# Two-layer float32 block pair on one core: heads in pairs with row-tiled scores, spatial gating's last products moved into the heads' first steps

## The reference

```python
# first kind, l = 0, 1: beside a differential attention, eight heads of 64 over 1024 tokens, two key/value heads
q = apply_rope(rms_norm(bq)); k = apply_rope(rms_norm(bk))
ob = gqa_attention(q, k, bv)              # softmax(q k^T / 8) v, no mask, four query heads on one key head
yb = ob * silu(bg)

# second kind, l = 0, 1
y_a = silu(z_a) * (u * (einsum('gts,bcsgd->bctgd', tril(w_s), layer_norm(v)) + b_s))   # spatial gating
score = sum_h w_idx * relu(q_idx k_idx^T / 8)       # which keys a query may see
idx = top_k(score, 256)                             # ties go to the lower index
y_b = silu(z_b) * sparse_attention                  # eight heads of 64, one key/value head, the chosen keys only
```

## Time and profile before

| | us |
|---|---|
| median of the runs | 3182.53 (3180.21 to 3183.30, 3 runs) |
| profiled execution | 3185.18 |
| its span (first to last instruction) | 3183.4 |
| PE busy in the span | 2747.1 (86%) |
| DVE busy | 2070.8 (65%) |
| ACT busy | 1594.8 (50%) |
| POOL busy | 1154.7 (36%) |
| mean granted TensorE clock | 0.933 of full |
| unmasked heads, layers 0 and 1 | 569.1 to 785.9, 1431.8 to 1646.0 |
| end of the search and gating, layers 0 and 1 | 2152 to 2199, 2866 to 2912.5 |
| masked heads, layers 0 and 1 | 2199.0 to 2355.6, 2912.8 to 3070.5 |

### The profile page before, as it was taken

One profiled execution on the slowest core, in us unless ns is written; L12 is line 12 of the kernel. 1 busy time (PEld: TensorE's weight loads), 2 busy tenths in 40 slices (PEclk: granted clock), 3 DMA queues, 4 the chain that ended last, 5 costly groups with the idle time before them and its releaser, 6 DMA issues. The chain is left out here.

```text
span 3183.4 us, 40934 instructions
## 1 busy us (share of the span) xinstructions
PE 2747.1 (86%) x13680; PEld 2191.3 (69%) x13680; DVE 2070.8 (65%) x4254; ACT 1594.8 (50%) x3093; POOL 1154.7 (36%) x981
## 2 busy tenths in 40 slices
PE   6999798898979997889989797996889697996887
PEld 5877566677868775657777575775767575775766
DVE  4372387688434624858874348898867358898756
ACT  3221376688422114757873216674864316674861
POOL 0100277455001003864540001985631001985631
PEclk9999899899989997999999898998999899998989
DMA  4343110100324321001023100110022100110022
GB/s 123 118 137 103 73 39 7 40 1 28 119 72 144 123 70 54 24 5 39 1 72 108 53 20 24 47 44 24 1 110 76 63 24 17 47 44 24 1 87 80
DMA packets 90751, 181.92 MB, mean 57 GB/s; under 512 B 12552, under 2 KB 27912, under 8 KB 90504
## 3 DMA queue, kind: packets, MB, share of 16 engines
q1 hardware_dynamic: 74124, 150.69, 14.7%
q10 hardware_dynamic: 16416, 28.61, 3.0%
HBM read 149.87 MB, written 33.33 MB: 58 GB/s over the span
## 5 line engine op out<-in xcount | busy, mean ns | idle before, releaser
L681 PE MATMUL ps<-w_hi,hh 128*128 128x512 f32 (+1 forms) x640 | 243.1, 380 | 22.2 <-DVE w_lo L566 10.1
L1263 POOL TENSOR_SCALAR a_prob<-a_prob,a_ratio 128x1024 f32<-128x1024 f32 x64 | 72.1, 1126 | 505.5 <-DVE a_ratio L1222 505.5
L681 PE MATMUL ps<-w_lo,hh 128*128 128x512 f32 (+1 forms) x640 | 241.0, 377 | 0.0
L1685 PE MATMUL ps<-o_w_hi,hh 128*128 128x512 f32 x512 | 211.7, 414 | 32.2 <-DVE o_w_lo L1609 32.2
L681 PE MATMUL ps<-w_hi,hl 128*128 128x512 f32 (+1 forms) x640 | 239.3, 374 | 0.0
L2151 DVE TENSOR_SCALAR_CACHE_REDUCE select_rows<-masks,select_cuts 128x1024 bf16<-128x1024 int16 (+7 forms) x264 | 229.7, 873 | 0.2
L1685 PE MATMUL ps<-o_w_lo,hh 128*128 128x512 f32 x512 | 207.5, 405 | 0.0
L1685 PE MATMUL ps<-o_w_hi,hl 128*128 128x512 f32 x512 | 207.1, 405 | 0.0
L960 POOL TENSOR_SCALAR b_prob<-b_prob,b_recip 128x1024 f32<-128x1024 f32 x128 | 144.2, 1127 | 172.5 <-DVE b_recip L925 169.9
L1665 POOL TENSOR_TENSOR o_rstd<-o_rstd,nhalf 128x1 f32<-128x1 f32 x56 | 46.6, 833 | 423.8 <-DVE o_rstd L1546 245.3
L1211 DVE CUSTOM_DVE_ANT_0 a_prob<-ps,a_bias 128x1024 f32<-128x1024 f32 x128 | 151.6, 1222 | 57.9 <-PE ps L1348 57.9
(11 more groups left out here) (354 smaller groups left out, 8350.3 us busy)
## 6 DMA issues: line engine op xcount, KB each, us to landing
w_early<-in_w_in SPq DMA_DIRECT2D x108, 256.0 KB, 2.8
ada_w<-in_w_ada ACTq DMA_DIRECT2D x96, 256.0 KB, 2.7
w_raw<-in_w_in SPq DMA_DIRECT2D x84, 256.0 KB, 2.8
...
```

What stands on the lines that cost most here:

```text
L681: mm = nc.tensor.matmul(o, lhs, rhs, start=(k == 0 and i == 0), stop=(k == K - 1 and i == 2))
L1685: mm = nc.tensor.matmul(o, lhs, rhs, start=(k == 0 and i == 0), stop=(k == K - 1 and i == 2))
```

## The change

`heads_phase` now takes two heads at a time. The blocks of the two heads alternate: block g is query tile g%16//2 of head g%2 of its pair.

- Queries are turned as they lie (a tile of 128 columns holds both heads), keys are staged twice side by side by ACT; ACT writes the high half of the turned tile and DVE the low half, for both sides. So there are four query stacks instead of eight, and the staging of queries by ACT and DVE is gone.
- Scores of a pair of blocks: three products (high-high, high-low, low-high) for each head and bank with 64 rows each, heads in alternation: twelve instead of eight with 128 rows. Head 0 goes to banks 0 and 1, head 1 to banks 2 and 3. They are issued in odd steps for the next two blocks and wait until both blocks before are shifted.
- In the unmasked form too, DVE now writes the negated scores to SBUF (with a zero added in place of a mask), and ACT's exponential reads them there.
- `plan`: turned tiles start at step 4n+8 and stand only in even steps, all tiles of two steps together (four in a step, or two). With three banks the fourth turn of a step waits for the low half of the first. The ring holds 16 rows. A group is closed at step 4n+13 (4n+10 before), the loop ends at NB+14 (NB+11).

In `select_project_phase` the tie order is 3, 2, 7, 4, 6, 5, and the wait for the gates stands before the third; DVE multiplies chunk U from PSUM into the gates after the third (eight of 128x512), PE's spatial products follow, and ACT copies them into `v`. Bias and last product are given to `heads_phase` as `gating`: POOL does two products of 128x512 ahead of the scaling in each of its steps 1 to 8. `v` itself is lent as four rows of the ring, and DVE waits at block 12 until all eight gatings are done.

```diff
-    QB, RING, SLOTS, NS = 4, 10, 4, 4
+    QB, RING, SLOTS, NS = 4, 16, 4, 4
+    TURN, READ = 8, 13
...
         for j in range(tiles(n)):
-            plan[QB * n + 5 + j // per].append(("attn", n, j))
+            plan[QB * n + TURN + j // per // 2 * 2].append(("attn", n, j))
...
                 def shift(g):
-                    dve.wait_ge(scored, g + 1)
+                    dve.wait_ge(scored, g // 2 + 1)
...
+                    if g >= RING:
+                        dve.wait_ge(turned, last_tile[group_with(g - RING)])
+                    elif g == RING - len(lent):
+                        dve.wait_ge(mixed, len(gating))
+                    added = (row_view(bias(query_tile(g)), g) if causal
+                             else zero[:, 0:1].unsqueeze(2).broadcast_to([P, 2, BANK]))
+                    nc.vector.tensor_tensor_reduce(out=row_view(prob(g), g), in0=score_view(g), in1=added,
+                                                   scale=-1.0, scalar=3.0e38, op0=ALU.add, op1=ALU.min,
+                                                   accum_out=nm[:, g % NS:g % NS + 1]).then_inc(shifted, 1)
...
+                def gate(z):
+                    total, added, y = gating[z]
+                    nc.gpsimd.tensor_tensor(total, total, added, ALU.add).then_inc(biased, 1)
+                    pool.wait_ge(biased, z + 1)
+                    nc.gpsimd.tensor_tensor(y, y, total, ALU.mult).then_inc(mixed, 1)
...
                     if 1 <= g <= NB:
+                        if g <= len(gating):
+                            gate(g - 1)
                         b = g - 1
...
                     if g >= 2:
-                        pe.wait_ge(shifted if causal else exped, g - 1)
+                        pe.wait_ge(shifted, g)
...
-                        nc.tensor.matmul(o, q, where["k", group[h], "hh"][:, cols], start=True, stop=False)
-                        mm = nc.tensor.matmul(o, q, where["k", group[h], "ll"][:, cols], start=False, stop=True)
+                        for i, (qe, ke) in enumerate([(0, 0), (0, 1), (1, 0)]):
+                            for m in range(2):
+                                rows = slice(m * HD, (m + 1) * HD)
+                                mm = nc.tensor.matmul(ps[:, 2 * m + b, 0:w], q_st[rows, qe, tok], k_st[rows, ke, cols],
+                                                      start=(i == 0), stop=(i == 2))
...
-                    if 0 <= g + 1 < NB:
+                    if g % 2 and 0 <= g + 1 < NB:
                         scores(g + 1)
...
-                dve.wait_ge(gated, 4 * T)
-                for i, qb in enumerate(ORDER):
+                for i, qb in enumerate([3, 2, 7, 4, 6, 5]):
...
+                    if i == 2:
+                        after(issued[0])
+                        dve.wait_ge(gated, 4 * T)
...
-                    if i >= 2:
-                        add_bias(2 * i - 4)
-                        add_bias(2 * i - 3)
+                    if i == 2:
+                        for z in range(8):
+                            weigh_gate(z)
...
-                pool.wait_ge(gated, 4 * T)
-                for z in range(8):
-                    weigh_gate(z)
-                for z in range(8):
-                    mix(z)
```

340 lines of the change are left out of this document (137 added, 203 removed).

## The result

The changed kernel takes 3278.2 us (median of 4 runs, 3275.8 to 3281.7), the kernel before 3181.4 on the same chip: ratio 1.0304, 95% interval 1.0289 to 1.0320. It is slower, as forecast, but by 97 us and not by 49, and outside the range. The profiled execution spans 3280.0 us.

What follows compares the result with a forecast made beforehand. PE was taken to lead the unmasked heads, no engine to be full in the masked, DVE to pace the search's end. 17.4 + 22 - 15 = 24.4 us a layer, 48.8 for two: 3231 us, range 3188 to 3264.

Steps and rivals of the forecast that it cites:

- The ring: Unmasked pairs: waits close a loop, 5.98 us through scores, shift and exponential, or 6.01 through PE's products and turns.
- Turned tiles four at a time: Heads: the fourth turn in three banks waits for a low half; held decisive, mean 6.2 us an unmasked pair.
- Closing pairs: Unmasked heads: every second pair's next products also wait for the closing copies, 6.44 us a pair.
- The start of the unmasked heads: Unmasked heads: start 8.9 us in place of 8.2, then first four pairs 21.6 in place of 22.2.
- The end of the unmasked heads: Unmasked heads from block 62 to the phase's end: 32.4 us in place of 22.5 a layer.
- The masked steady part: Masked heads: later pairs of heads some 37 us each in place of 34.8, +6.6 us a layer for three.
- Gating: Start of masked heads: POOL's two products before each of scalings 0 to 7 delay block 16, +7.3 us a layer.
- Rival (2): Masked heads: POOL's gating is hidden behind other waits, -7.3 us a layer, 3216 us; chance 0.11.
- End of the search: Between projection and masked heads: less DVE idle time, POOL's products and stalls gone, -15 us a layer.
- rival (3): End of the search: DVE's stalls stay, of another origin, -6.4 us a layer in place of -15, 3248 us; chance 0.11.
- Rival (1): Heads: PE sets the pace, an unmasked pair takes PE's own 5.28 us, 3160 us, faster; chance 0.13.
- Rival (4): Steady part: PE's waits drop its granted clock from 2.4 to 1.2 GHz, over 3290 us; chance 0.03.

Runs made afterwards that it cites:

- e1: Changed kernel with turned tiles two (or one) in every step, not four (or two) in every second: 3165.4 us, ratio 0.9947.
- e2: Changed kernel with the fourth turned tile of a step put behind the next scores, its products a step later: 3172.7 us, ratio 0.9970.
- e15: Changed kernel with the second closing copy made by DVE, ahead of its low halves, in place of ACT: 3247.9 us, ratio 1.0201.
- e10: Changed kernel with the gatings left out of the masked heads, and DVE's wait for them too: 3261.2 us, ratio 1.0237.
- e9: Changed kernel with 14 more POOL products of 128x512 from SBUF while DVE does the last ties: 3298.5 us, ratio 1.0357.
- e6: e1 with masked heads one at a time as before, gatings on POOL; unmasked heads stay in pairs: 3157.2 us, ratio 0.9913.

## Why the prediction was wrong, point by point

**The ring was right, its size nearly.** (It is the second of the two rings, as the sums had it, 6.01 against 5.98; that so small a difference picked the right one is luck.) "Turned tiles four at a time" was named as decisive, and e1 and e2 show it. The plain pairs are 6.16 us apart in place of 6.01: the fourth turn and the change of form took 0.59 and not the 0.50 I took, the four tiles' products 1.95 and not 1.92. Closing pairs were right with 6.44 (measured 6.46 to 6.62). Over 26 pairs with the stacks that is 3.2 us a layer (168.4 against 165.2).

**The start of the unmasked heads was mis-sized.** I had 21.6 us for the first four pairs, taken from the earlier trace rows, and 6.2 for the fifth, 27.8; it took 31.8. The first pairs took 23.7, since DVE also splits the values there, and the first pair with turns 8.2, with a stack's turn ahead of its own and scores that still take 2.73 us, near the lower clock's price (2.93 in the earlier trace rows). +4.0.

**The end of the unmasked heads.** 35.4 against 32.4, +3.0. Its four steps take 23.9 us from fourth turn to fourth turn (4.66, 8.15, 4.65, 6.47) where the term had 21.8; the 8.15 holds products at the 1.2 GHz level, 1.7 us over the 6.47 at the upper one, and the term had nothing for that. Behind the last turn no experiment parts the rest. The masked end runs at the lower level in part too (0.81 granted in the window above).

**The masked steady part, with the end behind it, is the step that failed.** I gave the four short-score steps 4.9, 5.1, 5.7 and 5.5 us and made the three later pairs of heads 37 us each. They took 40.4, 39.5 and, with the end, 68.9 where 61.7 were forecast. The four short-score steps took 5.8, 5.8, 5.2 and 6.0, 1.5 us more than forecast in sum; the four others took 16.8, where the forecast left 15.8 for them. What is missing in the short steps is the full price of the two closing copies on ACT, which stand behind the fourth high half and ahead of the next products; I had them in the unmasked ring, and in the masked steps only in part. e15 moves one of them away, and the first two of these pairs of heads come to 37.4 and 37.5, the forecast's length, and the end gets 3.6 shorter. Steady part and end together are some 13 us a layer, more than half of the miss. One step of 7.3 to 7.55 us in each layer, with products at the 1.2 GHz level, is the clock's, 1.6 us. The 2 to 3 us that e15 wins in each pair of heads agree with this account; that all of the 13 us hang on the copies isn't shown.

**Gating: right.** Forecast +7.3, measured +7.8 to block 16; left out (e10), block 16 comes 9.4 us earlier and the masked heads get 5.9 and 8.2 us shorter in the two layers. Rival (2) is ruled out. One reading beside this term has no row: the earlier trace rows show a shift of 1.23 us and no line of POOL. It stands in the same trace, where POOL works from 509.86 us on for 2.41 us and a shift of 1.23 us starts at 510.17.

**End of the search: right.** Forecast -15, measured -14.2, and the parts fit: 5.9 us less idle time where 6.4 were forecast, 8.2 less work where it was 9. The stall of 1.06 us that carried the term is 0.75 to 0.96 for ten of e9's eleven longer instructions, and rival (3), stalls of another origin, is ruled out by it. The estimate that stood beside it from the Trainium skill (SBUF — State Buffer, Who interferes with whom), a whole product of 1.3 us for a blocked instruction, is not what e9's scans show: 0.94 to 0.96.

**Rival (1)** did not happen in the changed kernel, but it describes e1: with the ring cut, PE does set the pace at 5.4 us. It came to 3165 and not to 3160. **Rival (4)** is ruled out for the steady part without a mask (granted clock 1.00), and holds for single steps of the masked heads and of the ends.

What stays open: why the same masked step runs at the upper level in most pairs of heads and at the lower in others, and whether a masked form in pairs could reach the single heads. e1 stays 3.8 us behind e6 in layer 0 (160.3 and 156.5) and 6.5 in layer 1, and most of it is the longer end: behind block 62 e1 takes 24.1 and 25.3 us, e6 20.5 and 20.0, while from block 0 to block 62 they differ by 0.2 and 1.1.
